# Moving the last activation pair's sums, its split and four tile loads to later units of the down projection

## What is computed

```python
h2 = rmsnorm(x, norm_ffn[l])
g = causal_dwconv(h2 @ ffn_w_gate[l], ffn_conv_w[l])      # width 3
x = x + (jax.nn.silu(g) * (h2 @ ffn_w_up[l])) @ ffn_w_down[l]
```

## Time and profile before

| what | value |
|---|---|
| runs | 2112.37, 2112.72, 2119.51 us (median 2112.72) |
| profiled execution | 2116.9 us, of which the span is 2115.1 us |
| PE busy | 2104.3 us, 99% of the span |
| DVE, ACT, POOL busy | 1555.0, 1008.6, 1276.4 us |
| DMA | 308.76 MB, mean 146 GB/s |
| granted TensorE clock | mean 1.00 |

### The profile page before, as it was taken

How to read it: one execution, slowest core, us unless ns; L and a number is a source line. 1 busy time by engine, 2 the same in 40 slices (tenths; PEclk the granted TensorE clock), 3 DMA queues, 4 the chain that set the end, 5 groups by cost and what they waited for, 6 DMA issues and landing times.

```text
span 2115.1 us, 34610 instructions
## 1 busy us (share of the span) xinstructions
PE 2104.3 (99%) x11476; PEld 1782.6 (84%) x11476; DVE 1555.0 (74%) x2756; ACT 1008.6 (48%) x1468; POOL 1276.4 (60%) x731
## 2 busy tenths in 40 slices
PE   9999999999999999999999999999999999999999
PEld 6777777887888888888888888888888899888888
DVE  6489565457663226888888888888888768988987
ACT  6343344434433446545545555555555544444443
POOL 5345334444545656667767767767767676666665
PEclk9999999999999999999999999999999999999999
DMA  6224123233333443344544544544544766655743
GB/s 210 84 74 126 63 69 100 95 105 102 103 99 125 146 145 134 136 164 140 169 154 145 171 144 144 169 152 141 166 151 148 260 222 209 212 187 189 234 130 125
DMA packets 150119, 308.76 MB, mean 146 GB/s; under 512 B 13272, under 2 KB 54424, under 8 KB 149880
## 3 DMA queue, kind: packets, MB, share of 16 engines
q1 hardware_dynamic: 103568, 250.39, 35.3%
q10 hardware_dynamic: 46440, 56.94, 8.6%
HBM read 261.64 MB, written 45.51 MB: 145 GB/s over the span
## 4 chain that ended last, share of the span: by engine, by line
PE 92%; DVE 6%; issue 1%; ACT 0%; DMA 0%; ACTq 0%; SPq 0%; DVEq 0%
PE ps L870 38%; PE ps L869 20%; PE ps L681 10%; PE ps L683 9%; PE ps L682 9%; PE ps L876 1%; PE ps L878 1%; PE ps L877 1%; DVE work L1458 1%; DVE work L1457 1%; DVE work L1361 1%; PE ps L777 1%; DVE work L1360 1%; PE ps L763 0%; PE ps L749 0%
## 5 line engine op out<-in xcount | busy, mean ns | idle before, releaser
L870 PE MATMUL ps<-comb,fhi 128*128 128x512 f32 x3360 | 1180.5, 394 | 0.0
L869 PE MATMUL ps<-comb,flo 128*128 128x256 f32 x3360 | 943.6, 281 | 0.0
L870 PEld LDWEIGHTS ps<-comb,fhi 128*128 128x128 f32 x3360 | 629.8, 187 | 143.9
L629 POOL TENSOR_TENSOR flo<-raw,fhi 128x1024 fp32r<-128x1024 f32 (+2 forms) x252 | 485.0, 1934 | 361.8 <-ACT fhi L1208 361.0
L869 PEld LDWEIGHTS ps<-comb,flo 128*128 128x128 f32 x3360 | 634.4, 189 | 5.6 <-DVE ps L1817 2.2
L599 POOL TENSOR_TENSOR wlo<-raw,whi 128x512 fp32r<-128x512 f32 x260 | 361.4, 1403 | 394.9 <-ACT whi L988 344.1
L629 POOL TENSOR_TENSOR flo<-sum,fhi 128x1024 fp32r<-128x1024 f32 (+2 forms) x168 | 324.0, 1936 | 41.0 <-ACT fhi L1208 40.5
L1208 ACT ACTIVATE fhi<-ps 128x1024 fp32r<-128x1024 f32 (+2 forms) x168 | 141.7, 844 | 420.1 <-DVE ps L1699 242.5
L681 PE MATMUL ps<-hhi,whi 128*128 128x512 f32 x784 | 317.3, 405 | 2.4 <-DVE hlo L1608 2.4
L683 PE MATMUL ps<-hlo,whi 128*128 128x512 f32 x784 | 306.4, 391 | 0.0
L682 PE MATMUL ps<-hhi,wlo 128*128 128x512 f32 x784 | 305.7, 390 | 0.0
(11 more groups left out here) (246 smaller groups left out, 2799.2 us busy)
## 6 DMA issues: line engine op xcount, KB each, us to landing
raw<-w_gu SPq DMA_DIRECT2D x176, 512.0 KB, 3.4
raw<-w_in SPq DMA_DIRECT2D x196, 256.0 KB, 3.2
raw<-w_dn SPq DMA_DIRECT2D x96, 256.0 KB, 2.9
raw<-w_dn SPq DMA_DIRECT2D x64, 320.0 KB, 3.1
act_hi<-thi ACTq DMA_DIRECT2D x20, 896.0 KB, 4.2
act_lo<-tlo ACTq DMA_DIRECT2D x20, 896.0 KB, 8.2
raw<-w_out SPq DMA_DIRECT2D x64, 256.0 KB, 3.2
comb<-act_hi SPq DMA_DIRECT2D x21, 512.0 KB, 3.9
```

Source lines behind the costliest of these rows:

```text
L629: nc.gpsimd.tensor_tensor(flo[s][:, 0:w], src[:, 0:w], fhi[s][:, 0:w].bitcast(F32), ALU.subtract).then_inc(f_lo_pool, 1)
L869: nc.tensor.matmul(dst[:, 0:HT], flo[s][:, w], both[:, HI, :], start=fresh and k == 0, stop=False, skip_group_check=True)
L870: ins = nc.tensor.matmul(dst, fhi[s][:, w], both, start=False, stop=k == n - 1, skip_group_check=True)
```

## The change

1. DVE makes the four sums of the last pair one each in units 45, 46 and 47 (behind the second addition) and the fourth at the end of unit 47, in place of all in unit 44.
2. ACT and POOL split the last pair in unit 48 in place of unit 45.
3. ACT issues the loads of positions 5 and 6 of chunk 0 in unit 44 behind the first tap and behind high 4, in place of behind high 2 and high 3.
4. Output pairs 4 and 5 go to `x2d` and to `upv`/`sqsum`, pairs 6 and 7 to tiles 4 to 7 of `x2b`. SP loads pairs 4 and 5 behind A12 of unit 47, now on `f_act >= 44`, and pairs 6 and 7 behind A12 of unit 49, now on `t_lo >= 22` (before: behind A12 of unit 48).

```diff
 # SP
-                if p == NPAIR - 1:
+                if p == 5:
                     sp_.dma_start(upv[:, :], x2_rows[2 * p]).then_inc(x2_loaded[p], 16)
                     sp_.dma_start(sqsum[:, :], x2_rows[2 * p + 1]).then_inc(x2_loaded[p], 16)
                     return
-                dst = {1: x2b[:, 0:2, :], 2: x2b[:, 2:4, :], 3: x2c[:, :, :], 4: x2b[:, 4:6, :], 5: x2b[:, 6:8, :], 6: x2d[:, :, :]}[p]
+                dst = {1: x2b[:, 0:2, :], 2: x2b[:, 2:4, :], 3: x2c[:, :, :], 4: x2d[:, :, :], 6: x2b[:, 4:6, :], 7: x2b[:, 6:8, :]}[p]
...
                 if u == FT + 3:
-                    sp_.wait_ge(t_lo, FP)
+                    sp_.wait_ge(f_act, FT)
                     load_x2(4)
                     load_x2(5)
-                if u == FT + 4:
-                    sp_.wait_ge(f_act, FT)
+                if u == FT + 5:
+                    sp_.wait_ge(t_lo, FP)
                     load_x2(6)
                     load_x2(7)
...
 # POOL
-                if lane(n) % 2 == 1 and n != 1 and (gate_up(n) or n == FT + 1):
+                if lane(n) % 2 == 1 and n != 1 and gate_up(n) or n == FT + 4:
...
 # ACT, unit(n)
-                if n == FT:
-                    load_chunk(sc, 0, 5)
                 sc.wait_ge(loaded12, lin(n, 16, 16))
                 high_unit(n, 3, raw12)
-                if n == FT:
-                    load_chunk(sc, 0, 6)
...
                     first_tap(step(n, -1))
+                if n == FT:
+                    load_chunk(sc, 0, 5)
                 sc.wait_ge(sum3_ready, lin(n, 1, 1))
                 high_unit(n, 4, sum3)
...
+                if n == FT:
+                    load_chunk(sc, 0, 6)
-                if lane(n) % 2 == 1 and n != 1 and (gate_up(n) or n == FT + 1):
+                if lane(n) % 2 == 1 and n != 1 and gate_up(n) or n == FT + 4:
...
 # DVE
+            def last_sum(i):
+                buf = act[(FP - 1) % 2]
+                to, a, b = ((2, 0, 1), (4, 6, 0), (3, 6, 2), (5, 7, 3))[i]
+                ve.wait_ge(f_act, FT)
+                ve.wait_ge(t_sum, 4 * (FP - 1) + (0, 0, 1, 3)[i])
+                V.tensor_tensor(buf[:, to, :], buf[:, a, :], buf[:, b, :], ALU.subtract).then_inc(t_sum, 1)
...
                     tap(n - 1, 1)
                     tap(n - 1, 2)
+                if 1 <= v <= 3:
+                    last_sum(v - 1)
...
-                if tail:
-                    act_sums(n, 0)
...
-                if tail:
-                    act_sums(n, 1)
...
-                if tail:
-                    act_sums(n, 2)
+                if v == 3:
+                    last_sum(3)
```

More of the change, by code:

```diff
@@ L456, in x2_tile @@
         def x2_tile(d):
-            return (x2a[:, d, :] if d < 2 else x2b[:, d - 2, :] if d < 6 else x2c[:, d - 6, :] if d < 8 else x2b[:, d - 4, :] if d < 12
-                    else x2d[:, d - 12, :] if d < 14 else upv[:, :] if d == 14 else sqsum[:, :])
+            return (x2a[:, d, :] if d < 2 else x2b[:, d - 2, :] if d < 6 else x2c[:, d - 6, :] if d < 8 else x2d[:, d - 8, :] if d < 10
+                    else upv[:, :] if d == 10 else sqsum[:, :] if d == 11 else x2b[:, d - 8, :])
         def pieces(c, b):
@@ L639, in unit @@
                     low_unit(step(n, 1), 0, raw11)
-                if lane(n) % 2 == 1 and n != 1 and (gate_up(n) or n == FT + 1):
-                    m = lin(n, 1, -3) // 2 if isinstance(n, int) else 2 * n[0] + (n[1] - 3) // 2
+                if lane(n) % 2 == 1 and n != 1 and gate_up(n) or n == FT + 4:
+                    m = FP - 1 if n == FT + 4 else (n - 3) // 2 if isinstance(n, int) else 2 * n[0] + (n[1] - 3) // 2
                     pool.wait_ge(t_hi, m + 1)
-                    if n == FT + 1:
+                    if n == FT + 4:
                         last = act[(FP - 1) % 2]
@@ L1262, in unit @@
                     load_chunk(sc, 0, 0)
-                if lane(n) % 2 == 1 and n != 1 and (gate_up(n) or n == FT + 1):
-                    m = pair_of(n)
+                if n == FT:
+                    load_chunk(sc, 0, 6)
+                if lane(n) % 2 == 1 and n != 1 and gate_up(n) or n == FT + 4:
+                    m = FP - 1 if n == FT + 4 else pair_of(n)
                     sc.wait_ge(t_sum, 4 * m + 4)
-                    if n == FT + 1:
+                    if n == FT + 4:
                         last = act[(FP - 1) % 2]
@@ L1858, in down_unit @@
                 if v < NPAIR:
-                    ve.wait_ge(x2_loaded[v], 16 if v < NPAIR - 1 else 32)
+                    ve.wait_ge(x2_loaded[v], 32 if v == 5 else 16)
                 accumulate(v, 1, 0, late, xbank(n))
```

## The result

| | before | after |
|---|---|---|
| median of 12 runs each | 2112.81 us (2109.29 to 2119.51) | 2124.17 us (2119.52 to 2128.65) |
| profiled execution | 2116.9 us, span 2115.1 | 2121.0 us, span 2119.2 |
| mean granted clock | 1.00 | 0.997 |

The ratio is 1.0049, 95% interval 1.0037 to 1.0062: +10.4 us, between +7.8 and +13.1. The forecast was +9.3 us.

A forecast was written before the change was run, and what follows sets the result against it. PE, busy 99% of the span, was taken as the bound. A 7.6 us stall plus 1.9 for the clock less 0.2 gained in unit 44 gave +9.3 us on the 2112.7 median: 2122.0 us, range 2117.0 to 2125.5.

The forecast's parts named there:

- The new wait of SP: In unit 49, behind A12, SP would stand from 1719.4 until the split ends at 1729.3, holding unit 50's weights.
- The burst: Loads queued behind SP's wait, through A21 of unit 50: 9.15 us from first issue, so A21 lands at 1738.5.
- Copy, high part, low part, PE: Unit 49: chain from ACT's copy of A21 to the end of POOL's low part, 2.5 us, holding PE's position 5.
- The clock: PE's gap in unit 49 makes the granted clock fall; coming back costs 1.9 us, bounds 0 and 3.8.
- the clock holds: Rival: the gap in unit 49 leaves the clock alone, total 7.4 us (2120.1); chance 0.17, shared with faster-draining loads.
- long cold restart: Rival: PE stays at 1.2 GHz longer in unit 49, restart over 3.2 us, slower by over 0.5%; chance 0.20.
- Unit 44: PE's two stalls there, 2.07 us in all; landing of position 6's activations taken as unchanged, so 0.2 us gained.
- Harmless wait: Rival: split done before SP arrives, or A21 of unit 50 has slack; only unit 44 counts, 2110.6 to 2112.5; chance 0.04.
- The sums at nothing: The four sums in units 45 to 47 cost nothing: DVE mostly waits about 1.0 us there, against 0.41 a sum.

## Why the prediction was right, and where its sizes were off

**Right in kind and near in size.** +9.3 us forecast, +10.4 (7.8 to 13.1) measured, +8.2, +7.6 and +8.1 in the ledgers of three executions. The kernel with the wait one unit later shows that the place of the wait is the cause of the loss.

- *The new wait of SP*: as forecast. 13.1 us behind the start of unit 48 were taken over from the earlier trace rows for the end of the split; it came 13.0 behind (unit 48 starts 2.93 us earlier than in the earlier trace rows).
- *The burst*: 9.15 us were taken from the same burst in unit 47 (1709.80 less 1700.63 is 9.17); 8.51, 8.60 and 8.17 were measured. The bound from below was 7.4. The stretch from first issue to copy had 308 GB/s over 9.2 us there, which is 2.8 MB, and 296 over 8.5 us, 2.5 MB, here. The burst itself is 2.1 MB. So the row of unit 47 carried 0.3 MB more of other traffic, 1 us at that rate: **the term was oversized by 0.6 to 1.0 us, as a whole stretch was taken over with the work that shared it.** The likely share is A12 of unit 47, 0.26 MB: it went out 0.4 us ahead of that burst, while A12 of unit 49 had gone out 10 us ahead of this one. No run took it away, so this is argued and not shown. The Trainium skill (DMA: Bandwidth & Descriptors, "Anatomy of one DMA") fits one transfer issued by GpSimd as 2.0 us plus bytes over 436 GB/s; an estimate by that fit is 6.8 us for the burst and 2.6 us for the lone block. The trace disagrees for the burst, and comes near it for the lone block, with 2.72 us from issue to copy.
- *Copy, high part, low part, PE*: 2.5 us forecast, 1734.81 to 1737.36 is 2.55 us.
- *The clock*: 1.9 us forecast from the start of the span, 2.6, 1.75 and 1.9 measured. That start shows six slow matmuls, but the profile's stretches give a granted clock of 1.00 from 0 to 7 us, so it did not show the half clock itself; that the two costs are near each other is in part luck. By the stretches, the clock stayed at the half for 10.2, 6.8 and 6.8 us in the three executions, of which 5.7, 3.8 and 4.1 us fell on PE at work. Of the rivals, "the clock holds" fell in every gap of 2.8 us or more and held only at 1.0 us; "long cold restart" needed 3.2 us and did not come. The Trainium skill (TensorE: Matmul & The Clock Gate, "Part 1") says that the moment of rise varies from run to run. The traces agree: 14 to 26 matmuls at half clock in six executions, and 26, 17 and 18 in three of the same kernel.
- *Unit 44*: **the step that was mis-sized.** "I take the landing as unchanged and the gain as 0.2 us": the gain was 1.2, 1.1 and 0.3 in the three executions of the changed kernel, 0.5 with the wait in unit 50. The part of DVE was read rightly (0.3 us). But the landing did not stay in the first two: in the first trace the low part of position 6 went out only 0.2 us earlier against the start of the unit and landed 0.9 us earlier (6.8 us from issue to landing in place of 7.5). In the third it took 8.2 us and landed as late as before. ACT's long issue (2.28 us in the earlier trace rows) came back on the load of position 5, and shorter:

```profile
1672.13 0.63 ACT L1208 ACTIVATE fhi<-raw 128x512 fp32r<-128x512 f32 x1 [0.24 <-PE ps L870]
...
1672.67 0.68 ACT L1231 ACTIVATE ps<-gpad,pc 128x512 f32<-128x512 f32 x1
1672.68 1.28 ACTq L480 DMA_DIRECT2D comb<-act_lo  x1
1674.07 0.63 ACT L1208 ACTIVATE fhi<-sum 128x512 fp32r<-128x512 f32 x1 [0.72 <-PE ps L878]
1674.14 0.34 ACTq L480 DMA_DIRECT2D comb<-act_hi  x1
1674.51 0.48 ACTq L480 DMA_DIRECT2D comb<-act_lo  x1
```

  (ACT and its issues after, unit 44, as in the earlier trace rows; the unit starts at 1671.87.) The first tap runs directly behind the high part, no longer 2.33 us later, so POOL's stall is gone. That is the new order of the issues and not the sums. On which load the long issue falls goes with the gain in all the traces that leave SP's queue of unit 45 alone: on position 5's load (this one, and five more, 1.2 to 1.6 us long) 0.9 to 1.2 us are gained, on position 6's (0.7 to 1.3 us long, three traces) 0.3 to 0.5, and in the two kernels with the old order it is on position 6's too, 2.3 and 2.5 us long, and the gain is 0 and 0.1. That is a correlation over eleven traces; what makes an issue long, and on which load, was not tried.
- *Harmless wait*: fell. Where it is harmless is one unit later: SP gets there behind the split.
- *The sums at nothing*: held. In the same places behind the second addition PE waits for nothing.

In the first ledger the sizes were off by -0.8 us for the gap, -1.0 for unit 44 and +0.7 for the clock: 1.1 us below the forecast. The timing came out 1.1 us above it. That the forecast lies so near to both is in part luck. Between the ledgers (+7.6 to +8.2) and the centres of the two timings (+10.4, +10.0) 2 us stay open. Both intervals take in +8.1 and +8.2, and +7.6 lies just below the first. Whether anything outside units 44 to 49 adds to it can't be told: in the three traces of the changed kernel unit 44 starts at 1671.87, 1674.06 and 1680.80, ahead of everything that was changed.

No kernel that ran was measured to beat the one before. The parts without the misplaced wait won at most 1.2 us in unit 44 in any trace, which is less than the scatter of the runs.

## What to carry to other kernels

A wait in a queue that issues loads costs what stands behind it, not what it guards: name the first load behind it that is needed soon, and count the megabytes that will go out ahead of it once the wait ends (here 1.0 us for the hold and 3.0 to 4.0 us for each MB). When a row of the trace prices a burst, divide by what the DMAs moved in that stretch before it is taken over to another place. And where two releasers of a stall lie tenths apart, taking one of them away shows only the other; ask what each part of the edit does to both.

## What the runs showed of the hardware

- The granted clock fell, by the share of the slice in which it did, 2.1, 3.7 and 3.6 us after PE went idle in the changed kernel, and 4.0 us after with the chunk loads first. With one pair queued it fell 2.8 us after, when PE had been back at work for 0.2 us, and with the pairs behind A21 5.0 us after, when PE had been back for 1.1 us. An idle time of 2.6 us was enough once, and one of 0.9 us was not. So a gap can be paid for after it has ended.
- Issuing one 384 KB load takes 0.33 to 0.57 us on ACT's queue around unit 44, but in each of the 13 traces one of unit 44's four took longer: 0.7 us once, 1.2 to 2.5 us in the others.
- Executions of the same kernel run the same matmuls at slightly different rates in stretches where PE waits for nothing and the granted clock is 1.00: the 60 matmuls shown with the ledger took 10.40 us in the changed kernel's first trace and 10.60 in its third and in the one before. What sets the rate was not tried. Over a span that comes to several microseconds of either sign, and one trace beside another can't show a change of that size except step by step.
